# Expert stage: later scatters, and gathers just ahead of the steps that read them

## The chip, the cores and the metric

The program runs on one core of a Trainium2 chip. The metric is the device time of one execution in microseconds, less is better. TensorE multiplies matrices (in the profile PE, its weight loads PEld), VectorE (DVE) and ScalarE (ACT) move results out of the matmul banks (PSUM, eight of them, `PS`) and do the arithmetic between the matmuls, GpSimd (POOL) helps in the dense part, and SyncE (SP) issues the loads from memory. Each has its own list of instructions and they meet through semaphores only. All loads are carried by the same 16 DMA engines.

## What is computed

Two blocks in a row on 512 tokens of width 1024, all in float32. The first block has a gated recurrence, an attention and two SwiGLU layers, the second three attention branches and then a layer of experts. Only the last one is touched by the change:

```python
def expert_choice_ffn(x, w_router, w_gate_up, w_down):
    B, T, D = x.shape
    cap = EC_CAPACITY_FACTOR * T // N_EXPERTS        # 2 * 512 // 16 = 64
    logits = jnp.einsum('btd,de->bte', x, w_router, preferred_element_type=jnp.float32)
    aff = jax.nn.softmax(logits, axis=-1)
    gate, idx = lax.top_k(jnp.swapaxes(aff, 1, 2), cap)
    bidx = jnp.arange(B)[:, None, None]
    xs = x[bidx, idx]
    h = jnp.einsum('becd,edf->becf', xs, w_gate_up)
    hg, hu = jnp.split(h, 2, axis=-1)
    ye = jnp.einsum('becf,efd->becd', jax.nn.silu(hg) * hu, w_down)
    ye = ye * gate[..., None].astype(ye.dtype)
    return jnp.zeros_like(x).at[bidx, idx].add(ye)
```

Each of the 16 experts takes its 64 best tokens. Its weights are 1024 x 2048 (gate and up) and 1024 x 1024 (down), 12.6 MB for an expert, 201 MB for all. The layer's output is added to its scaled input and normalised, and that is the result.

## The kernel before

`experts_order` writes the order of the stage as a list of steps; each engine's program walks through the same list and does its part of each step, so one list sets the order on all engines. `claim` takes the PSUM bank that has been free longest, `release` says which event frees it, and a matmul that writes a claimed bank first waits for that event.

The experts run as eight pairs, i = 0 to 7, and two pairs share a group q = i // 2 of four experts. For a pair:

- `gather` (q, d): the tokens of the group's four experts, for 128 of the 1024 features, as a product of the normalised input (high part XH and low part XL, L2575 and L2576) with a one-hot matrix (the tile named PE): 16 matmuls on TensorE. VectorE scales the result into `XS[:, d]` (L2121). XS serves both pairs of the group, so for q > 0 this write waits until step `up` (2q - 1, d) has read the old one. `one_hot` (VectorE, L2114) writes the matrix of the next group.
- `up` (i, k), k = 0 to 7: 16 matmuls (L2591) with `XS[:, k]` as weights over two loads of 1 MB. Then `silu` (ScalarE) and the product (VectorE, L2127) into HG; `h_turn` transposes it (L2227) and ScalarE copies it back (L1351).
- `slot_gates` (L2605) for an even pair, the gate values of the group.
- `down` (i, k), k = 0 to 3: 16 matmuls (L2631) over two loads of 1 MB. `y_out` takes the result in a high and a low part, YOH (ScalarE) and YOL (VectorE, L2154).
- `scatter` (i, tb, h): 4 blocks of tokens by 2 halves, two matmuls each (L2660, L2661) with the transposed one-hot matrix GT, added on VectorE into X (L2148, L2150; for some L2140 is the addition of `back`). `scatter_t` makes GT: transposes of the tile PE for the group (L2227), copied by ScalarE.
- `back`, in pair 4 alone: the layer's input is transposed back and added to X.

The order around the change: pair 0 does its gathers two ahead of the `up` that reads them, two before up 0 and a pair of them behind up 1, up 3 and up 5. In pairs 1, 3 and 5 all eight gathers of the next group stand in twos behind up 1, 3, 5 and 7. The eight scatters of pair i - 1 stand between up 7 and `h_turn` of pair i. `scatter_t` stands behind down 0 of the even pairs. In pair 7 the scatters of pair 6 stand between the ups.

The weights are 196 loads that SyncE issues in their order (L1246; the last ones L1249 and L1250), 24 for a pair. There are 19 slots of 1 MB (`SL`, and the tiles C and X, which lie in other tiles' place) at first and 16 later. A load into a slot that was used waits for the `up` or `down` that read it (`ex("w", ...)`); nothing else in this list waits for other engines once the stage runs.

```python
                if j in last_in:
                    e.wait_ge(*ex("w", last_in[j] // 2))
                last_in[j] = i
```

Of the kernel before, what the change touches and what calls it, by code (L numbers as in the profile page):

```python
# [742 lines left out]
def experts_order(o, us):  # L743
# [63 lines left out]
    def gather(q, d):  # L807
        o.claim("ga", q, d)
        o.add("gather", q, d)
        o.release(("ga", q, d), "xs", q, d)  # L810

    def scatter(i, *tbs):
        for tb in tbs:
            for h in range(2):
                o.claim("sc", i, tb, h)
                o.add("scatter", i, tb, h)
                o.release(("sc", i, tb, h), "xup", "sc", i, tb, h)

    def back(c):
        if c == 0:  # L820
            o.add("ident")
        if c:
            o.claim("xb", c - 1)
            o.add("back_turn", c - 1)
            o.release(("xb", c - 1), "xup", "back", c - 1)
        if c < DC:
            o.claim("xr", c)
            o.add("back", c)
            o.release(("xr", c), "back", c)

    def carry(tb, *halves):
        for h in halves:
            o.claim("fin", tb, h)
            o.add("carry", tb, h)

    for i in range(8):
        q = i // 2
        for n in range(4):
            o.claim("h", i, n)
        if i == 0:  # L840
            o.add("one_hot", 0)
            gather(0, 0)
            gather(0, 1)
        for k in range(8):
            o.add("up", i, k)
            if i % 2 and i < 7 and k % 2:
                gather(q + 1, k - 1)
                gather(q + 1, k)
            if i == 0 and k % 2 and k < 7:
                gather(0, k + 1)  # L850
                gather(0, k + 2)
            if i == 7 and 1 <= k < 5:
                scatter(6, k - 1)
                o.add("halves", k - 1)
            elif i == 7 and k >= 5 and k < 7:
                carry(k - 5, 0, 1)
            elif i == NBACK:
                back(k)
        if i == NBACK:
            back(DC)  # L860
        for n in range(2):
            o.add("silu", i, n)
            o.release(("h", i, n), "silu", i, n)
            o.release(("h", i, 2 + n), "mul", i, n)
        if i == 0:
            o.add("alpha")
        elif i < 7:
            scatter(i - 1, *range(4))
        for half in range(2):
            o.claim("ht", i, half)  # L870
            o.add("h_turn", i, half)
            o.release(("ht", i, half), "turn", "ht", i, half)
            if i % 2 == 0 and half == 0:
                o.claim("gw", q)
                o.add("slot_gates", q)
                o.release(("gw", q), "xs", "gw", q)
        for n in range(2):
            o.claim("y", i, n)
        def y_out(n):
            o.add("y_out", i, n)  # L880
            o.release(("y", i, n), "lo", "y2", i, n)

        if i == 7:
            break
        for k in range(4):
            o.add("down", i, k)
            if i % 2 == 0 and k == 0:
                for j in range(2):
                    o.claim("gt", "e", q, j)
                    o.add("scatter_t", q, j)  # L890
                    o.release(("gt", "e", q, j), "turn", "gt", q, j)
                if q < 3:
                    o.add("one_hot", q + 1)
        y_out(0)
        y_out(1)

# [53 lines left out]
def whole_order():  # L950
    o = Order()
    rglru_order(o)
    ffn_order(o, 0, 2)
    sb_order(o)
    ffn_order(o, 1, 4)
    us = mixer2_order(o)
    o.n_dense = len(o.units)
    experts_order(o, us)
    return o
# [1867 lines left out]
```

## Time and profile before

| | us |
|---|---|
| runs of the kernel | 2118.39, 2118.40, 2119.78 |
| median | 2118.4 |
| the profiled execution, its time | 2120.52 |
| the profiled execution, its span | 2118.7 |
| TensorE busy | 2086.6 (98% of the span) |
| VectorE busy | 1023.1 (48%) |
| ScalarE busy | 750.2 (35%) |
| GpSimd busy | 146.4 (7%) |
| DMA, bytes moved | 352.09 MB |

The span runs from the first to the last instruction that the profiler saw; the time has some 1.8 us more around it. The dense part takes the first 1650 us or so, the experts run from there to 2105 us, and the last microseconds are the normalisation and the output. A busy TensorE is not one at its peak, since its matmuls are pipelined and their ends are modelled.

### The profile page before, as it was taken

The numbers are of one execution on the slowest core, as the hardware profiler recorded it, in microseconds if no ns is written. First come the engines' busy times: TensorE is split into PE (matmuls) and PEld (weight loads), VectorE is DVE, ScalarE is ACT, GpSimd is POOL, SyncE is SP. The second block draws the span as 40 slices with busy tenths as digits, with TensorE's granted clock in tenths as the row PEclk, the third lists the DMA queues.
The fourth block names the chain that finished last, engine by engine and source line by source line (L and its number), as shares of the span: only waits on it lengthen the run. The fifth ranks groups of instructions, "written<-read, shape, count | busy, mean of one in ns | idle before, by whom it ended". The sixth has DMA issues, their size and how long they took to land.

```text
span 2118.7 us, 24857 instructions
## 1 busy us (share of the span) xinstructions
PE 2086.6 (98%) x10137; PEld 1517.1 (72%) x10137; DVE 1023.1 (48%) x1515; ACT 750.2 (35%) x1076; POOL 146.4 (7%) x149
## 2 busy tenths in 40 slices
PE   9999999999999999999999999999999999999998
PEld 7878888888777778888888877777787544444433
DVE  7875433445666664434446656564464312122123
ACT  7774322323455543222334456533333100011012
POOL 0220000001000020000001010062101000000000
PEclk9999999999999999999999999999999999999999
DMA  6233223324211123233233322242236999999996
GB/s 218 75 104 110 83 83 124 100 69 121 70 60 59 61 92 105 69 123 99 82 88 119 115 60 77 60 89 72 73 110 231 401 426 412 427 427 426 426 427 275
DMA packets 88944, 352.09 MB, mean 166 GB/s; under 512 B 9472, under 2 KB 24064, under 8 KB 64512
## 3 DMA queue, kind: packets, MB, share of 16 engines
q1 hardware_dynamic: 83856, 342.48, 43.6%
q0 software_dynamic: 2192, 2.63, 1.0%
q10 hardware_dynamic: 2784, 5.41, 0.7%
q8 instruction: 81, 1.33, 0.3%
q14 instruction: 31, 0.25, 0.0%
HBM read 347.06 MB, written 2.10 MB: 165 GB/s over the span
## 4 chain that ended last, share of the span: by engine, by line
PE 86%; DVE 5%; DMA 4%; ACT 3%; issue 2%; POOL 0%; ACTq 0%; DVEq 0%; SPq 0%; POOLq 0%
PE PS L2184 20%; PE PS L2185 19%; PE PS L2186 19%; PE PS L2591 9%; PE PS L2631 4%; DMA SL<-in_wgu_dram 3%; PE PS L2227 2%; DMA SL<-in_wdn_dram 1%; DVE WL L1664 1%; PE PS L2301 1%; PE PS L2575 1%; PE PS L2325 1%; PE PS L2315 1%; PE PS L2576 1%; DVE XC L1731 1%
## 5 line engine op out<-in xcount | busy, mean ns | idle before, releaser
L2184 PE MATMUL PS<-HH,WH 128*128 128x512 f32 x1392 | 553.9, 398 | 3.0 <-DVE HL L1704 2.2
L2186 PE MATMUL PS<-HH,WL 128*128 128x512 f32 x1392 | 543.0, 390 | 0.0
L2185 PE MATMUL PS<-HL,WH 128*128 128x512 f32 x1392 | 542.6, 390 | 0.0
L1664 DVE TENSOR_TENSOR WL<-RAW,WH 128x1024 fp32r<-128x1024 f32 (+4 forms) x302 | 343.5, 1138 | 294.6 <-ACT WH L1340 293.7
L1340 ACT ACTIVATE WH<-RAW 128x1024 fp32r<-128x1024 f32 (+4 forms) x302 | 286.5, 951 | 308.5 <-PE PS L2186 278.3
L2184 PEld LDWEIGHTS PS<-HH,WH 128*128 128x128 f32 x1392 | 261.7, 188 | 69.1 <-issue 10.3
L2186 PEld LDWEIGHTS PS<-HH,WL 128*128 128x128 f32 x1392 | 261.7, 188 | 55.6
L2185 PEld LDWEIGHTS PS<-HL,WH 128*128 128x128 f32 x1392 | 262.0, 188 | 52.9 <-issue 1.0
L2591 PE MATMUL PS<-SL,XS 128*64 128x512 f32 x928 | 220.8, 595 | 6.4 <-DMA SL<-in_wgu_dram 5.8
L2591 PEld LDWEIGHTS PS<-SL,XS 128*64 128x64 f32 x928 | 70.4, 137 | 135.7 <-issue 133.7
L2186 PE MATMUL PS<-MH,WL 128*128 128x512 f32 x352 | 136.9, 389 | 0.0
L2184 PE MATMUL PS<-MH,WH 128*128 128x512 f32 x352 | 136.9, 389 | 0.0
L2185 PE MATMUL PS<-ML,WH 128*128 128x512 f32 x352 | 136.9, 389 | 0.0
L1674 DVE TENSOR_TENSOR U<-PS,RS 128x512 f32<-128x512 f32 x44 | 30.4, 691 | 106.2 <-PE PS L2186 106.2
L1449 ACT ACTIVATE MH<-U 128x512 fp32r<-128x512 f32 x44 | 27.9, 633 | 141.2 <-DVE U L1787 141.2
L1613 ACT ACTIVATE HG<-PS 128x512 f32<-128x512 f32 x8 | 4.8, 596 | 204.0 <-PE PS L2591 204.0
L2184 PEld LDWEIGHTS PS<-MH,WH 128*128 128x128 f32 x352 | 66.1, 188 | 13.8
L2186 PEld LDWEIGHTS PS<-MH,WL 128*128 128x128 f32 x352 | 66.1, 188 | 13.7
L2185 PEld LDWEIGHTS PS<-ML,WH 128*128 128x128 f32 x352 | 66.1, 188 | 13.6
L2121 DVE TENSOR_SCALAR XS<-PS,V 128x256 f32<-128x256 f32 x32 | 17.4, 544 | 116.7 <-PE PS L2576 116.7
L1776 DVE TENSOR_TENSOR X<-X,PS 128x512 f32<-128x512 f32 x56 | 38.0, 684 | 55.9 <-PE PS L2186 55.9
L1323 POOL COPY SA<-SQ 128x512 f32<-128x512 f32 x4 | 2.7, 674 | 846.9 <-ACT SQ L1372 846.9
(375 smaller groups left out, 2740.5 us busy)
## 6 DMA issues: line engine op xcount, KB each, us to landing
SL<-in_wgu_dram SPq DMA_DIRECT2D x116, 1024.0 KB, 21.8
SL<-in_wdn_dram SPq DMA_DIRECT2D x55, 1024.0 KB, 24.8
RAW<-in_w_dram SPq DMA_DIRECT2D x46, 512.0 KB, 3.4
RAW<-in_wg_dram SPq DMA_DIRECT2D x44, 512.0 KB, 3.4
RAW<-in_wu_dram SPq DMA_DIRECT2D x44, 512.0 KB, 3.4
RAW<-in_wd_dram SPq DMA_DIRECT2D x32, 384.0 KB, 3.1
RAW<-in_wqkv_dram SPq DMA_DIRECT2D x24, 512.0 KB, 3.5
RAW<-in_wd_dram SPq DMA_DIRECT2D x32, 320.0 KB, 2.9
```

What stands on the lines that cost most here:

```text
L1340: e.activation(WH[u % NSPL][:, 0:n], RAW[raw_of[u]][:, 0:n], ACT.Copy).then_inc(*whs.did("u", u))
L1449: e.activation(MH[l][:, f, :], U1[l][:, z, :], ACT.Copy).then_inc(*hi.did("m", l, half, f))
L1664: e.tensor_tensor(wl, raw, wh.bitcast(F), ALU.subtract).then_inc(*wlo.did("u", u))
L1674: e.tensor_tensor(dst, src, r, ALU.mult).then_inc(*scaled.did(*event))
L1731: e.scalar_tensor_tensor(out=XC[s][:, :], in0=XB[p][:, 1 + j:T + 1 + j], scalar=vec("cw", 8 * j + c), in1=XC[s][:, :], op0=ALU.mult, op1=A ...
L1776: e.tensor_tensor(X[:, c, :], X[:, c, :], bank(*key), ALU.add).then_inc(*xup.did(*key))
L2184: e.matmul(out, wh[:, w], xh, start=k == 0, stop=False)
L2185: e.matmul(out, wh[:, w], xl, start=False, stop=False)
L2186: m = e.matmul(out, wl[:, w], xh, start=False, stop=k == g.total - 1)
L2227: m = e.transpose(bank(*key)[:, 128 * j:128 * j + 128], src, ident)
L2591: m = e.matmul(bank("h", i, n)[64 * e2:64 * e2 + 64, :], XS[:, k, x0:x0 + 64], SL[slot(l0 + e2)][:, 512 * n:512 * n + 512], start=k == 0, ...
L2631: m = e.matmul(bank("y", i, n)[64 * e2:64 * e2 + 64, :], HT[k // 2][:, 2 * (k % 2) + f, 64 * e2:64 * e2 + 64], SL[slot(l0 + e2)][:, 1024 * ...
```

## The change

Three things move in the list of steps; no instruction is added or taken away, and the banks that are claimed shift with the order.

- Gathers: in pairs 1, 3 and 5 only gathers 0 and 1 of the next group are left, behind up 1. The other six stand in the following even pair, in twos behind its ups 1, 3 and 5, as in pair 0.
- Scatters: those of pair i - 1, for i = 1 to 6, stand behind down 0 (block 0), down 1 (block 1) and down 2 (blocks 2 and 3) of pair i, where they stood ahead of its `h_turn`.
- `scatter_t` and the next `one_hot`: for pairs 2, 4 and 6 behind down 3, where they stood behind down 0.

```diff
@@ -843,12 +843,12 @@
             gather(0, 1)
         for k in range(8):
             o.add("up", i, k)
-            if i % 2 and i < 7 and k % 2:
-                gather(q + 1, k - 1)
-                gather(q + 1, k)
-            if i == 0 and k % 2 and k < 7:
-                gather(0, k + 1)
-                gather(0, k + 2)
+            if i % 2 and i < 7 and k == 1:
+                gather(q + 1, 0)
+                gather(q + 1, 1)
+            if i % 2 == 0 and k % 2 and k < 7:
+                gather(q, k + 1)
+                gather(q, k + 2)
             if i == 7 and 1 <= k < 5:
                 scatter(6, k - 1)
                 o.add("halves", k - 1)
@@ -864,8 +864,6 @@
             o.release(("h", i, 2 + n), "mul", i, n)
         if i == 0:
             o.add("alpha")
-        elif i < 7:
-            scatter(i - 1, *range(4))
         for half in range(2):
             o.claim("ht", i, half)
             o.add("h_turn", i, half)
@@ -884,13 +882,15 @@
             break
         for k in range(4):
             o.add("down", i, k)
-            if i % 2 == 0 and k == 0:
+            if i % 2 == 0 and k == (3 if i else 0):
                 for j in range(2):
                     o.claim("gt", "e", q, j)
                     o.add("scatter_t", q, j)
                     o.release(("gt", "e", q, j), "turn", "gt", q, j)
                 if q < 3:
                     o.add("one_hot", q + 1)
+            if 0 < i < 7 and k < 3:
+                scatter(i - 1, *((0,), (1,), (2, 3))[k])
         y_out(0)
         y_out(1)
```

TensorE in pair 1, from the last scatter to the first matmul of pair 2, before. Ahead of these rows stand seven more scatters and, ahead of them, gathers 6 and 7. The counts of L2591 and L2631 are half of the matmuls, so x8 is one up or down; the two rows of L2631 are the downs 0 and 1, then 2 and 3:

```order
L2660 MATMUL PS<-YOH,GT 128x512
L2661 MATMUL PS<-YOL,GT 128x512
L2227 MATMUL PS<-C,HG 128x128 x4
L2227 MATMUL PS<-C 128x128 x4
L2631 MATMUL PS<-SL,HG 64x512 x16
L2631 MATMUL PS<-SL,C 64x512 x16
L2591 MATMUL PS<-SL,XS 64x512
```

The same place now, from the last ups of pair 1 to down 1:

```order
L2591 MATMUL PS<-SL,XS 64x512 x24
L2591 MATMUL PS<-X,XS 64x512 x8
L2227 MATMUL PS<-C,HG 128x128 x4
L2227 MATMUL PS<-C 128x128 x4
L2631 MATMUL PS<-SL,HG 64x512 x8
L2660 MATMUL PS<-YOH,GT 128x512
L2661 MATMUL PS<-YOL,GT 128x512
L2660 MATMUL PS<-YOH,GT 128x512
L2661 MATMUL PS<-YOL,GT 128x512
L2631 MATMUL PS<-SL,HG 64x512 x8
```

Nothing stands any more between the last up and the turns of HG, and the scatters have gone in between the downs.

VectorE from the end of pair 0 to the end of pair 2 (L2121 the gathers, L2127 the products, L2148 and L2150 the scatters, L2131 the gates, L2114 the one-hot matrix):

```order
-L2121 TENSOR_SCALAR XS<-PS,V 128x256 x8
+L2121 TENSOR_SCALAR XS<-PS,V 128x256 x2
 L2127 TENSOR_TENSOR HG<-HG,PS 128x512
 L2127 TENSOR_TENSOR C<-C,PS 128x512
 L2148 COPY X<-PS 128x4x128 x8
 L2154 SCALAR_TENSOR_TENSOR YOL<-PS,GA,YOH 128x512 x2
+L2121 TENSOR_SCALAR XS<-PS,V 128x256 x6
 L2127 TENSOR_TENSOR HG<-HG,PS 128x512
 L2127 TENSOR_TENSOR C<-C,PS 128x512
+L2131 COPY GA<-PS 128x2
 L2150 TENSOR_TENSOR X<-X,PS 128x4x128 x8
-L2131 COPY GA<-PS 128x2
```

Six of the eight XS writes move from pair 1 to pair 2, and the gates' copy stands ahead of the scatters. ScalarE's list and SyncE's are the same as before.

## Rows read from the trace of the kernel before

**Rows 1.** The page: span, forty slices, chain, a row of group 5.

```profile
span 2118.7 us, 24857 instructions
...
DMA  6233223324211123233233322242236999999996
GB/s 218 75 104 110 83 83 124 100 69 121 70 60 59 61 92 105 69 123 99 82 88 119 115 60 77 60 89 72 73 110 231 401 426 412 427 427 426 426 427 275
...
PE 86%; DVE 5%; DMA 4%; ACT 3%; issue 2%; POOL 0%; ACTq 0%; DVEq 0%; SPq 0%; POOLq 0%
...
L2121 DVE TENSOR_SCALAR XS<-PS,V 128x256 f32<-128x256 f32 x32 | 17.4, 544 | 116.7 <-PE PS L2576 116.7
```

**Rows 2.** Busy time by stretches; the last three columns are PEclk, DMA share, GB/s.

```profile
1750.00:1755.00 5.00, 4.79 (x26) 3.92 (x26) 5.00 (x9) 0.92 (x2) 0.00 (x0) 1.00 1.01 426
1755.00:1760.00 5.00, 5.00 (x26) 1.65 (x24) 1.47 (x3) 0.16 (x1) 0.00 (x0) 1.00 0.80 305
1760.00:1765.00 5.00, 5.00 (x26) 1.66 (x24) 0.00 (x0) 0.00 (x0) 0.00 (x0) 1.00 0.94 397
1765.00:1770.00 5.00, 5.00 (x26) 1.72 (x24) 0.55 (x1) 1.27 (x2) 0.00 (x0) 1.00 1.03 431
...
1765.00:2085.00 320.00, 311.44 (x1610) 136.87 (x1608) 67.23 (x109) 36.20 (x59) 0.00 (x0) 1.00 1.01 426
...
2005.00:2010.00 5.00, 3.79 (x19) 1.27 (x17) 0.00 (x0) 0.00 (x0) 0.00 (x0) 1.00 1.02 426
2015.00:2020.00 5.00, 3.79 (x20) 1.30 (x18) 0.00 (x0) 0.00 (x0) 0.00 (x0) 1.00 1.01 426
```

**Rows 3.** TensorE's timeline: start, duration, operation, in brackets the wait before it.

```profile
1912.91 0.63 PE L2227 MATMUL PS<-C 128*128 128x128 f32 x4 [0.96 <-ACT C L1639]
...
2003.95 3.65 PE L2591 MATMUL PS<-SL,XS 128*64 128x512 f32 x16 [0.65 <-DMA SL<-in_wgu_dram]
...
2013.79 3.65 PE L2591 MATMUL PS<-SL,XS 128*64 128x512 f32 x16 [1.32 <-DMA SL<-in_wgu_dram]
2018.65 3.65 PE L2591 MATMUL PS<-SL,XS 128*64 128x512 f32 x16 [1.21 <-DMA SL<-in_wgu_dram]
...
2082.68 0.72 PE L2227 MATMUL PS<-C 128*128 128x128 f32 x4 [0.82 <-DVE C L2127]
```

**Rows 4.** The chain that ended last, in the tail: start, duration, what.

```profile
2061.62 25.59 DMA SL<-in_wdn_dram
...
2087.34 3.65 PE PS L2631 x16
...
2092.13 5.30 PE PS L2645 x24
...
2099.02 1.89 PE PS L2645 x8
```

**Rows 5.** The same chain in pairs 0, 1 and 2.

```profile
1668.75 0.32 PE PS L2575
...
1670.84 7.02 PE PS L2591 x32
...
1713.56 6.87 PE PS L2591 x32
1720.42 0.32 PE PS L2575
...
1722.52 7.02 PE PS L2591 x32
...
1747.79 0.32 PE PS L2575
...
1753.57 0.48 PE PS L2227 x4
...
1754.73 13.95 PE PS L2631 x64
1768.68 27.47 PE PS L2591 x128
1796.15 0.43 PE PS L2660
...
1800.02 0.47 PE PS L2227 x4
1800.49 1.03 PE PS L2605 x32
...
1805.77 1.02 PE PS L2227 x8
```

**Rows 6.** Line L1246 in narrow windows: its loads, and their time to landing.

```profile
L1246 SPq DMA_DIRECT2D SL<-in_wgu_dram x2: 328/380/431, 1744.4 to 1744.8; - x2
...
DMA to landing us min/median/max: 13.0/14.0/15.0
...
L1246 SPq DMA_DIRECT2D SL<-in_wgu_dram x1: 327/327/327, 1758.4 to 1758.4; - x1
...
DMA to landing us min/median/max: 4.6/4.6/4.6
...
L1246 SPq DMA_DIRECT2D SL<-in_wgu_dram x1: 432/432/432, 1758.8 to 1758.8; - x1
...
DMA to landing us min/median/max: 6.7/6.7/6.7
...
L1246 SPq DMA_DIRECT2D SL<-in_wgu_dram x1: 327/327/327, 1761.9 to 1761.9; - x1
...
DMA to landing us min/median/max: 7.5/7.5/7.5
```

**Rows 7.** The same for later windows.

```profile
L1246 SPq DMA_DIRECT2D SL<-in_wgu_dram x8: 327/380/976, 1785.9 to 1796.6; - x8
...
DMA to landing us min/median/max: 17.8/21.1/24.3
...
L1246 SPq DMA_DIRECT2D SL<-in_wgu_dram x1: 328/328/328, 1805.8 to 1805.8; - x1
...
DMA to landing us min/median/max: 17.5/18.5/19.6
...
L1246 SPq DMA_DIRECT2D SL<-in_wgu_dram x1: 328/328/328, 1923.0 to 1923.0; - x1
...
DMA to landing us min/median/max: 18.0/18.0/18.0
```

## The prediction

> **What bounds the kernel now.** I read the page's slices first [rows 1]. TensorE is busy in nearly every slice, and the chain that ended last is 86% TensorE; that alone would say that every TensorE microsecond counts. But in the eight slices before the last, where the experts are, the DMA engines stand at 9 tenths or more and move 401 to 427 GB/s. There the chain is no longer a guide to what is scarce, so I looked at the stage in stretches of 5 us [rows 2]. From 1765 to 2085 us the mean is 426 GB/s with the DMA share at 1.01, and from 2004 us on TensorE waits for weights that have not landed: in 2005 to 2010 and in 2015 to 2020 it is busy 3.79 of 5 us, and four matmul groups in a row wait 0.65 to 1.32 us for a weight load [rows 3]. The tail hangs on that too: the chain goes through a load issued at 2061.62 that takes 25.59 us, and the step L2631 starts on it at 2087.34 [rows 4]. So the end of the program is the weight stream's end plus a tail that only starts with it. TensorE before about 2004 works off a store of landed weights; making it earlier there is worth nothing in itself. It is worth something only where its releases of slots let the stream go on.
>
> So the question is where the stream stands still for want of a free slot. After the change's first touched step (expert pair i=1, from 1713.56 on [rows 5]) there is one such place: 1755 to 1760 carries 305 GB/s and 1760 to 1765 carries 397, before and after it 426 and 431 [rows 2]. SyncE's queue says why [rows 6]: the load before the hole is issued at 1744.8 and lands 15.0 us later (1759.8), the next is issued only at 1758.4 and lands at 1763.0. It waits for the step down(1,0) to free its slot, and that step came late: up(1,7) ends at 1747.79, then stand one pair of gathers, eight scatters and the two turns, and down begins at 1754.73 [rows 5].
>
> **What the change does to the releases.** Per item, all on TensorE, durations from [rows 5]:
>
> Gathers. A pair of them is 1722.52 - 1720.42 = 2.10 us. Of the four pairs inside i=1 three move into i=2 (the same from 3 to 4 and from 5 to 6): 6.3 us leave the odd step and come back in the even one. Scatters. Eight are 3.9 us (1796.15 to 1800.02 in i=2), in i=1 they lie between the gathers and the turn at 1753.57. They move behind down 0, 1 and 2 as two, two and four, for i=1 to 6. The two scatter transposes of an even step, 1.0 us (L2227 x8 at 1805.77, [rows 5]), move behind down 3.
>
> The release that starved the stream: down(1,0) ended at 1754.73 + 3.5 = 1758.2. It loses 6.3 and 3.9 us ahead of it and ends at 1748.0. One thing is added: the scatters also covered the silu, the product and the transposes of HG. In i=7 no scatter stands there, and the second turn waits 0.82 us for VectorE's product [rows 3]; with the even steps slot_gates (1.03 us) stands between the turns and the chain shows no wait at i=0. So I add 0.8 us for each of i=1, 3 and 5: 1748.8, some 9.4 us earlier than before, and 11 us before the last issued load has landed (1759.8). From an empty queue a load takes 4.6 us from issue to landing [rows 6], so there is no hole left here.
>
> What is late next: with the same work in another order each release should be earlier or equal except for the added waits. I follow the sum: at the end of down(1,3) the scatters are done, so the lead is 6.3 - 0.8 = 5.5 us; each pair of gathers in i=2 takes 2.1 of it, so up(2,6) and up(2,7) are released 0.8 us later than before; then the eight scatters behind give 3.9 us of lead at down(2,0) and none at its end. After i=3 the lateness at the same points is 1.6, after i=5 2.4 us. The cover: the loads issued from 1785 to 1797 have 17.8 to 24.3 us until they land, the scarcest later ones are 17.5 (1806) and 18.0 us (1923) [rows 7]. Less 4.6 that is 13 us of work already queued against 2.4 us of lateness. No new hole.
>
> The new direct waits (a gather two steps ahead of the up that reads it, VectorE's XS write between them, 544 ns in [rows 1]) are already in i=0: there a pair of gathers takes 1668.75 to 1670.84, 2.09 us, the same as in i=1 where nobody reads it at once [rows 5]. I take them at zero; in i=4, where the back steps interleave with them, the nearest row is the 0.96 us wait for ScalarE [rows 3], so at most some 3 us for three pairs, hidden by the same 13 us. In i=6, where TensorE already waits for weights, it gets 6.3 us more: two ups and a pair take 7.02 + 2.10 = 9.1 us, four loads at 426 GB/s take 9.85 us (1.049 MB each), so the gathers fill part of the 1.2 us waits and delay nothing. On VectorE and ScalarE nothing is added, and SyncE's list of loads is the same.
>
> **What the hole is worth.** By bytes: (426 - 305) + (426 - 397) = 150 GB/s missing over 5 us, or 150 x 5 / 426 = 1.8 us. By landings, which is what TensorE waits for: 1759.8 to 1763.0 is 3.2 us where loads otherwise follow each other by 2.46 us, so 0.8 us. These are the two ends. The Trainium skill's page "DMA: Bandwidth & Descriptors", section "Queues, rings and completion order", says that one copy is split over up to 16 rings, each with its own engine, and so is not complete before its last part: engines that run ahead stand idle in the hole while the last ones still work. By that rule the value is 0.8 us, by the mean of the engines 1.8 us; no row here shows single engines. I take 1.0 us, nearer to the landing row, because landings release TensorE. One more row could belong to the restart: the load of 1758.8 lands at 1765.5, that of 1761.9 at 1769.4, 3.9 us apart instead of 2.46 [rows 6]. If this 1.4 us is a cost of starting again, it goes too, 2.2 to 3.2 us in all.
>
> **The sum.** Against the profiled execution (span 2118.7 us, time 2120.52, which is 1.8 us around the span and 2.1 above the median of the runs): 2120.5 - 1.0 = 2119.5. Against the median, 2118.4 - 1.0 = 2117.4 us, a change of 0.05%. A measurement of this kernel can tell about 0.2% (4.2 us) from no change, so I expect a time within that.
>
> **The rivals.**
> The hole was harmless or only moves: a small hole is paid back elsewhere, or a bank or SyncE holds the new issue. For: the byte rate before and after is already at its top. Against: nothing behind 1765 is below the mean, so what is lost there is not caught up. Time: 2118.4.
> The restart's 1.4 us belongs to it: 2118.4 - 2.7 = 2115.7. For: the long spacing stands two loads behind the hole. Against: it is one row.
> More of TensorE's lead counts, that is, TensorE and not the stream sets the end: then the change still gives nothing, since the work is the same and the added waits cost 3 x 0.8 us: 2120.8. The waits for weights in [rows 3] speak against it.
> Slower: the clock falls. TensorE gets to the store's end earlier (in i=5, since 6.3 - 2.4 = 3.9 us of work has left it by then) and waits more often in short pieces. If the granted clock drops to 1.2 GHz in the last steps, an up takes 7.0 instead of 3.5 us against loads that come every 4.9 us for two, and the lag no longer vanishes; with the tail's matmuls (3.65 + 5.30 + 1.89 + 2 us in [rows 4]) at half speed it costs some 13 us: 2131. It decides only if the low clock is there in the last ups of i=7, since a single slow one (3.5 us) is made good in three steps with 1.2 us to spare. Against: in 2005 to 2020 with TensorE at 3.79 of 5 us the granted clock is 1.00 [rows 2], and i=7 is not changed. The Trainium skill's page "TensorE: Matmul & The Clock Gate", section "HAM oscillation — how this bites in real kernels", says that matmul bursts parted by waits for DMA fall back to the half clock at each wait; that rule would make this rival the result, and no row of the weight-bound stretch shows it.
> Slower by a hole in i=4: it needs over 13 us of new waits there, for which I find no row; its price would be what exceeds them.
>
> **How the numbers follow.** Forecast (hole closed, 0.8 to 1.8 us) 60%; nothing gained 14%; restart included 15%; TensorE sets the end 5%; clock or another wait 3%; an unforeseen gain of over 4 us 3%. The runs shown spread from 2118.39 to 2119.78, 1.4 us upward. The first four lie between 2115.7 and 2120.8; the range takes the forecast's two ends, the restart's bound of 3.2 us and the spread above no change: 2115.0 to 2119.8. Within 0.2%: 94%; faster 3%; slower 3%.
>
> **What would show it.** In the changed profile the two stretches near 1755 to 1765 carry 426 GB/s; the load behind the one issued near 1744 is issued some 9 us earlier; a wait of about 0.8 us for VectorE's product appears at the second turn of i=1, 3 and 5; TensorE's first waits for weights come before 2004 and those in i=6 shrink; L2631's last wait ends near 2086.3 instead of 2087.34, and the tail from there is the same. Wrong would be a new stretch below 420 GB/s between 1765 and 2085, a granted clock under 1 there, or an end that moves by over 2 us with the same stream.

## The result and the profile after

| | before, us | changed, us |
|---|---|---|
| median of 12 runs each | 2118.79 | 2123.76 |
| lowest, highest | 2118.19, 2120.65 | 2122.41, 2126.47 |
| the profiled execution: time, span | 2120.52, 2118.7 | 2122.98, 2121.2 |

The changed kernel is 5.0 us slower: ratio 1.0022, 95% interval 1.0015 to 1.003. The prediction was 2117.4 us with a range of 2115.0 to 2119.8, so the time lies outside it and on the other side of no change.

The two profiled executions differ by only 2.5 us in span. Part of the difference lies ahead of the change: the first up of pair 1 starts at 1713.39 us in the kernel before and at 1711.83 in the changed one, 1.56 us earlier, in a stretch where both programs are the same. So I compare from there to the start of the first down of pair 7 (2083.33 before, 2086.33 now): 369.9 us before and 374.5 us now, 4.6 us more. Behind that point the changed kernel is 0.5 us shorter. Between the starts of the pairs' first ups, from TensorE's timeline:

| pair | 1 | 2 | 3 | 4 | 5 | 6 | 7, to its first down |
|---|---|---|---|---|---|---|---|
| before, us | 55.12 | 48.57 | 55.14 | 62.05 | 55.13 | 53.87 | 40.06 |
| changed, us | 50.63 | 56.40 | 50.69 | 72.20 | 50.68 | 56.40 | 37.49 |

The hole in the weight stream is gone. The same stretches as in [rows 2], the changed kernel (last three columns: granted clock, DMA share, GB/s), with two more that are read further down:

```profile
1755.00:1760.00 5.00, 5.00 (x24) 2.31 (x22) 2.31 (x4) 0.00 (x0) 0.00 (x0) 1.00 1.00 423
1760.00:1765.00 5.00, 5.00 (x26) 1.61 (x24) 1.58 (x3) 1.27 (x2) 0.00 (x0) 1.00 1.02 433
...
1765.00:2085.00 320.00, 315.75 (x1618) 135.87 (x1614) 70.29 (x113) 33.74 (x56) 0.00 (x0) 0.99 1.01 426
...
1915.00:1920.00 5.00, 2.57 (x43) 2.12 (x42) 1.96 (x4) 2.46 (x4) 0.00 (x0) 0.98 1.00 421
1920.00:1925.00 5.00, 5.00 (x20) 2.01 (x20) 0.16 (x1) 0.60 (x1) 0.00 (x0) 0.68 1.02 431
```

And the load that used to be late, which answers to [rows 6] (line L1246 in a narrow window of the changed kernel):

```profile
L1246 SPq DMA_DIRECT2D SL<-in_wgu_dram x1: 328/328/328, 1747.6 to 1747.6; - x1
...
DMA to landing us min/median/max: 13.7/13.7/13.7
```

It is issued at 1747.6, with the 1.56 us added 1749.1, where the forecast had 1748.8 and the kernel before 1758.4; it takes 13.7 us to land in place of 4.6, so there is queued work ahead of it. But TensorE no longer waits for any weights. Its waits from 1665 to 2090 us in the changed kernel (engine, line, waited for, total us, times, longest):

```profile
PE PS L2227 <- DVE C L2127: 3.3, 4, 0.8
PE PS L2227 <- DVE HG L2127: 1.5, 1, 1.5
PE PS L2227 <- ACT C L1639: 1.0, 1, 1.0
```

In the kernel before, the waits for weights alone were 6.5 us over this stage, four of them in [rows 3]; 6.0 us lie ahead of the first down of pair 7. The stream was the limit there; here it is TensorE's own list that sets the end, and every load lands before TensorE asks for it.

Where TensorE's time went is to be seen in the chain through the end of pair 1, against [rows 5] (start, duration, what; changed kernel):

```profile
1740.00 1.74 PE PS L2591 x8
...
1741.76 0.61 ACT C L1613
...
1742.39 0.70 DVE C L2127
...
1743.23 0.72 PE PS L2227 x4
1743.94 3.58 PE PS L2631 x16
1747.53 0.43 PE PS L2660
1747.96 0.24 PE PS L2661
1748.20 0.23 PE PS L2660
1748.43 0.24 PE PS L2661
1748.67 3.58 PE PS L2631 x16
...
1753.40 3.58 PE PS L2631 x16
1756.98 0.43 PE PS L2660
...
1759.05 3.58 PE PS L2631 x16
```

The first scatter matmul of each group takes 0.43 us of the chain, the next ones 0.23; each down takes 3.58, where four in a row took 13.95, or 3.49 each. From 1743.94 to the first up of pair 2 (1762.63) it is 18.69 us; before, the downs (13.95) and the scatters ahead of them (1749.91 to 1753.57, 3.66) took 17.61. That is 1.08 us more in an odd pair for work that is the same. In pair 2 it is 19.67 (1799.26 to 1818.93) against 15.06 + 3.87 = 18.93, 0.74 us more.

The second place is pair 4, in TensorE's, VectorE's and ScalarE's timeline of the changed kernel:

```profile
1915.23 0.78 ACT L1639 ACTIVATE C<-PS,LC 128x512 f32<-128x512 f32 x1 [4.24 <-PE PS L2671]
1916.15 0.63 PE L2227 MATMUL PS<-C 128*128 128x128 f32 x4 [0.96 <-ACT C L1639]
1916.82 0.69 DVE L2140 TENSOR_TENSOR X<-X,PS 128x512 f32<-128x512 f32 x1 [1.74 <-PE PS L2227]
1917.42 0.68 DVE L2127 TENSOR_TENSOR HG<-HG,PS 128x512 f32<-128x512 f32 x1
1918.25 0.72 PE L2227 MATMUL PS<-C,HG 128*128 128x128 f32 x4 [1.47 <-DVE HG L2127]
1919.95 1.13 PE L2227 MATMUL PS<-C 128*128 128x128 f32 x4
1921.02 1.12 PE L2631 MATMUL PS<-C,HG 128*64 128x512 f32 x1
1921.93 1.06 PE L2631 MATMUL PS<-C,HG 128*64 128x512 f32 x1
```

The last back step waits 0.96 us for ScalarE, as it did before. VectorE adds its result (L2140) and only then makes the product (L2127), and the turns, which nothing covers any more, wait for that, 1.47 us. Right behind these two waits the granted clock falls: 0.68 in the mean of 1920 to 1925, which holds a piece at the lower level, 1.2 GHz. The first matmuls of the down take 1.12 and 1.06 us in place of 0.59, and that down 4.67 us in place of 3.58.

**The account** (from the two traces, us of TensorE, from up(1,0) to down(7,0)). First TensorE's reserve in the kernel before, the time that it lost to the stream. Pair 6 has the same order there as pair 2 and took 53.87 us in place of 48.57; pair 7 took 40.06 us where the changed kernel, which waits for no weights, takes 37.49. That is 7.9 us: 6.0 us of waits, the rest in groups that run longer beside the waits. So without its waits the kernel before would need 362.1 us. The changed one takes 374.5, 12.4 us more: interrupted downs 3 x 1.08 + 3 x 0.74 = 5.5; the product's wait in pairs 1, 3 and 5, 3 x 0.83, less the 0.6 us that the downs waited there for HG before, 1.9; pair 4's wait 1.5; the low clock 1.5 (1.1 in the down, 0.4 in the turns); the turns, which no longer follow scatters and pay for their own first matmul, 1.4 (in pairs 1, 3 and 5 the two take 1.40 us in place of 1.11); 0.6 stays unassigned. The reserve takes up 7.9 of the 12.4, and what is left is the 4.6 between the traces (the terms are rounded); the runs have 5.0.

### The profile page after: what moved, and what is told of

It is laid out like the page before. It is cut to its first block, busy times and chain, and to the rows that moved or that the text cites. A ratio compares the mean times of both kernels' runs of the same rounds, so it can differ in the third digit from the quotient of the medians.

```text
span 2121.2 us, 24857 instructions
## 1 busy us (share of the span) xinstructions
PE 2091.8 (99%) x10137; PEld 1511.3 (71%) x10137; DVE 1025.6 (48%) x1515; ACT 750.2 (35%) x1076; POOL 146.3 (7%) x149
## 4 chain that ended last, share of the span: by engine, by line
PE 89%; DVE 5%; ACT 3%; issue 2%; DMA 1%; POOL 0%; ACTq 0%; DVEq 0%; SPq 0%; POOLq 0%
PE PS L2184 19%; PE PS L2186 19%; PE PS L2185 19%; PE PS L2591 11%; PE PS L2631 5%; PE PS L2227 2%; DVE WL L1664 1%; PE PS L2301 1%; PE PS L2660 1%; PE PS L2575 1%; PE PS L2325 1%; PE PS L2315 1%; PE PS L2576 1%; DVE XC L1731 1%; PE PS L2423 1%
## 5 line engine op out<-in xcount | busy, mean ns | idle before, releaser
L2591 PE MATMUL PS<-SL,XS 128*64 128x512 f32 x928 | 219.9, 595 | 0.0
L2591 PEld LDWEIGHTS PS<-SL,XS 128*64 128x64 f32 x928 | 68.6, 137 | 128.3 <-issue 126.4
L2184 PEld LDWEIGHTS PS<-MH,WH 128*128 128x128 f32 x352 | 66.1, 188 | 13.7
L2121 DVE TENSOR_SCALAR XS<-PS,V 128x256 f32<-128x256 f32 x32 | 17.4, 544 | 106.3 <-PE PS L2576 106.3
L1776 DVE TENSOR_TENSOR X<-X,PS 128x512 f32<-128x512 f32 x56 | 38.1, 684 | 55.9 <-PE PS L2186 55.9
L2150 DVE TENSOR_TENSOR X<-X,PS 128x512 f32<-128x512 f32 x48 | 30.4, 684 | 71.4 <-PE PS L2661 71.4
```

The source lines that it names most:

```text
L1776: e.tensor_tensor(X[:, c, :], X[:, c, :], bank(*key), ALU.add).then_inc(*xup.did(*key))
L2150: e.tensor_tensor(y, y, new, ALU.add).then_inc(*xup.did("sc", i, tb, h))
L2184: e.matmul(out, wh[:, w], xh, start=k == 0, stop=False)
L2591: m = e.matmul(bank("h", i, n)[64 * e2:64 * e2 + 64, :], XS[:, k, x0:x0 + 64], SL[slot(l0 + e2)][:, 512 * n:512 * n + 512], start=k == 0, ...
```

## Experiments

Each time is a median of 10 or 11 runs (five for the scatters alone), measured beside the kernel before on the same chip. The kernel before had a median of 2119.79, 2118.84 and 2119.18 us in the three comparisons, so a time is compared with the one of its own chip (that is what the ratio does) and not across chips. Where I give the length of "the stretch", it is the one from the first up of pair 1 to the first down of pair 7, from one trace of each kernel. From the expectations on record: pairs are numbered 0 to 7, and "the stream" is the order of weight loads.

### One half of the change at a time

The scatters alone:

```diff
-            if i % 2 and i < 7 and k == 1:
-                gather(q + 1, 0)
-                gather(q + 1, 1)
-            if i % 2 == 0 and k % 2 and k < 7:
-                gather(q, k + 1)
-                gather(q, k + 2)
+            if i % 2 and i < 7 and k % 2:
+                gather(q + 1, k - 1)
+                gather(q + 1, k)
+            if i == 0 and k % 2 and k < 7:
+                gather(0, k + 1)
+                gather(0, k + 2)
```

> Edit: from the changed kernel the gathers go back to where they were (eight in each of pairs 1, 3, 5); scatters and scatter_t stay in their new places. Theory A (the parts add up on TensorE, and the end comes late only when TensorE's sum passes the weight stream): the interrupted downs cost 1.06 us in an odd and 0.74 us in an even pair, the uncovered wait for the product 0.8 us in pairs 1, 3, 5: 7.8 us, but TensorE has 6.5 us of waits for weights in the kernel before and no gathers in pair 6, so the stream still sets the end. down(1,0) ends 3.1 us earlier, at 1755.1, so the hole of 1755 to 1765 shrinks to nearly nothing: 2116.6 to 2119 us, no slower than before. Theory B (the scatters between the downs are by themselves what costs, each microsecond on the path): 2118.8 + 5.4 + 2.4 = 2126.6, at least above 2122. Theory C (the gathers alone do the harm, by waits and the clock in pair 4): this kernel equals the one before, 2118.8.

Measured: 2126.52 us, ratio 1.0033 (1.0021 to 1.0046), worse than the whole change. Theory B's figure of 2126.6 is met, A's is missed. But B's sum is met by luck: it added 7.8 us, while TensorE got 15.9 us more (below) and its reserve took up 7.9. TensorE has no wait for weights left here either, and its stretch is 378.0 us. I had put the uncovered wait at 0.8 us a pair; it is longer when the last gathers stand right ahead of the turns. TensorE's waits from 1665 to 2090 us, and the chain at the end of pair 1:

```profile
PE PS L2227 <- DVE HG L2127: 5.4, 4, 1.5
...
1749.07 0.13 PE PS L2576
...
1749.23 0.54 DVE XS L2121
1749.77 0.60 DVE HG L2127
...
1750.51 0.73 PE PS L2227 x4
```

The product stands behind the last XS write on VectorE, and that stands behind the last gather: 5.4 us over four pairs. In pair 4 the clock stays at the lower level for longer than in the changed kernel (0.57 in 1920 to 1925, 0.75 in 1925 to 1930). Against the kernel before without its waits for weights (362.1) the stretch is 15.9 us longer; interruptions 5.5, waits 5.4 - 0.6, the clock 2.9 and the turns 1.4 explain 14.6 of them, 1.3 stays unassigned.

The gathers alone (the gather lines of the change, on the kernel before):

> Edit: the kernel before with only the gathers moved; scatters and scatter_t as before. Theory A (TensorE's sum against the stream): pair 4 costs some 3 us more (waits of 1.5 and 1.0 us and a granted clock of 0.68 in 1920 to 1925), pair 6 gets 6.3 us more, but the ups of pair 6 have room for that, and the end is set by the stream: 2116.6 to 2118.8, and the hole is closed. Theory B (scatters alone are the harm): 2116.6, the same number, with the clock at 1.00. Theory C (the gathers alone do the harm, by pair 4's waits and clock): 2122 or more, equal to the changed kernel. The profile decides between A and B by pair 4's length, 62.1 us before (1872.38 to 1934.43) and 72.1 us in the changed kernel.

Measured: 2118.07 us, ratio 0.9994 (0.9985 to 1.0003). The hole is closed, 428 GB/s in 1755 to 1760, the granted clock is 1.00 in 1915 to 1925, and waits for weights are there, 4.9 us for the ups. So the gathers do no harm to the time by themselves, not even between the back steps, and theory C falls. The scatters are where TensorE's added time comes from. A's mechanism stands for this kernel, but its expected clock drop did not come: the scatters ahead of the turns cover pair 4.

### The price of an interruption

```diff
-            if 0 < i < 7 and k < 3:
-                scatter(i - 1, *((0,), (1,), (2, 3))[k])
+            if 0 < i < 7 and k == 1:
+                scatter(i - 1, *range(4))
```

> Edit: the changed kernel with all eight scatters in one burst behind down 1 in place of two, two and four behind down 0, 1 and 2. Theory A (each place where TensorE leaves the downs for scatters and comes back costs some 0.3 us, and TensorE sets the end): two of three such places go in six pairs, 12 x 0.3 = 3.6 us: 2120.2 us, and the downs with scatters take 18.0 us in pair 1 instead of 18.7. Theory B (the interruption costs nothing, only the uncovered wait for the product counts): 2123.8, unchanged. Theory C (the gathers are the harm): 2123.8, unchanged.

Measured: 2120.33 us, ratio 1.0004 (0.9995 to 1.0013), as theory A had it. The stretch is 371.6 us, 2.9 less than in the changed kernel: five pairs are 0.72 to 0.80 us shorter each, and pair 4 is 0.85 us longer, because the clock stays low for longer there. The chain at the end of pair 1:

```profile
1743.74 7.02 PE PS L2631 x32
1750.76 0.43 PE PS L2660
1751.20 0.24 PE PS L2661
...
1754.65 7.02 PE PS L2631 x32
1761.67 3.43 PE PS L2591 x15
```

1743.74 to 1761.67 is 17.93 us against 18.69 with three interruptions: two fewer save 0.76, so 0.38 us each. It is a cost of leaving one kind of matmul for another and coming back, not of the scatters' work. The downs write 64 rows of a bank (`128*64` in the rows), the scatters 128. The Trainium skill, "TensorEngine Tiling (Array Packing)", section "Key Properties", says that a change of the tiling mode drains TensorE first. The longer first matmul agrees with it (0.43 in place of 0.23); no run here separates a drain from another cost at such a seam.

### The change at the hole alone

```diff
+            if i % 2 and i < 7 and (k % 2 if i > 1 else k == 1):
+                gather(q + 1, k - 1)
+                gather(q + 1, k)
+            if i in (0, 2) and k % 2 and k < 7:
+                gather(q, k + 1)
+                gather(q, k + 2)
...
-        elif i < 7:
+        elif 1 < i < 7:
             scatter(i - 1, *range(4))
...
+            if i == 1 and k == 1:
+                scatter(0, *range(4))
```

> Edit: the kernel before with the change at the hole alone: gathers 2 to 7 of the second group move from pair 1 to pair 2, the eight scatters of pair 0 stand in one burst behind down 1 of pair 1; all else, scatter_t too, as before. Theory A: down(1,0) ends some 9 us earlier, the hole is closed, which moved the landings by 2.2 us in the changed kernel, TensorE's sum grows by 1.5 us only and the stream sets the end: 2118.8 - 2.2 = 2116.6 us. Theory B (the end hangs on TensorE, not on the stream, and the hole has no worth): 2118.8 + 1.5 = 2120.3 us.

Measured: 2118.36 us, ratio 0.9993 (0.9984 to 1.0002). The same gathers without the scatters:

```diff
-            if i % 2 and i < 7 and k % 2:
+            if i % 2 and i < 7 and (k % 2 if i > 1 else k == 1):
                 gather(q + 1, k - 1)
                 gather(q + 1, k)
-            if i == 0 and k % 2 and k < 7:
-                gather(0, k + 1)
-                gather(0, k + 2)
+            if i in (0, 2) and k % 2 and k < 7:
+                gather(q, k + 1)
+                gather(q, k + 2)
```

> Edit: the kernel before with only gathers 2 to 7 of the second group moved from pair 1 to pair 2; scatters, scatter_t and all other pairs as before. Theory D: down(1,0) ends 6.3 us earlier, at 1752, well before the last issued load lands at 1759.8, so the hole is closed with no new wait and no interrupted downs, TensorE's sum grows by 0.2 us: 2118.8 - 1.8 to 2.2 = 2116.6 to 2117.0 us, as good as the kernel with both moves at pair 1. Rival (the hole has no worth at the end): 2118.8.

Measured: 2118.84 us, ratio 0.9998 (0.9989 to 1.0007), the same median as the kernel before. Both have whole streams at 1755 to 1765 (426 and 434 GB/s in the first five microseconds), both wait for weights later (4.2 and 4.8 us for the ups), and neither can be told from the kernel before. By the medians the hole was worth between nothing and 1.7 us at the end: these are the differences in the five kernels that close it and still wait for weights (the gathers alone, the two here, and two further down). The forecast's 1.0 is within that and not confirmed by it. The traces narrow it a little. The stretch is 369.1 to 369.2 us in four of these five kernels and 369.8 in the one with both moves at pair 1, against 369.9 in the kernel before and 370.1 in the one further down that keeps the hole. That is 0.7 to 1.0 us for the hole, with one case of 0.2 or 0.3, near the 0.8 that the forecast had from the landings; each is a single trace. The medians can't show it, since that first up starts anywhere from 1711.2 to 1714.4 us in the traces of the twelve kernels, though nothing ahead of it was changed.

### Is TensorE the bound?

Both kernels without the low part of the scatters of pairs 0 to 6:

```diff
-                    e.matmul(out, hot, YOH[:, cols], start=i < 7, stop=False, skip_group_check=True)
-                    e.matmul(out, hot, YOL[:, cols], start=False, stop=True, skip_group_check=True).then_inc(
-                        *ex.did("sc", i, tb, h))
+                    low = i == 7
+                    m = e.matmul(out, hot, YOH[:, cols], start=i < 7, stop=not low, skip_group_check=True)
+                    if low:
+                        m = e.matmul(out, hot, YOL[:, cols], start=False, stop=True, skip_group_check=True)
+                    m.then_inc(*ex.did("sc", i, tb, h))
```

> Edit: the changed kernel without the low parts in the scatters of pairs 0 to 6 (the L2661 matmul of 56 scatters is left out, so the sums lack the low part); order, loads, and the work of the other engines stay. It takes 56 x 0.23 = 12.9 us from TensorE. Theory D (in the changed kernel TensorE's own sum sets the end: it waits for no weights there, while the last loads land 0.9 to 1.0 us earlier than before, counted from the first expert load): TensorE falls below the stream and the stream sets the end, with the hole closed: 2118.8 - 2.2 = 2116.6 us, and waits for weights come back. Rival (the stream, or something behind it, sets the changed kernel's end): 2123.8, unchanged.

> Edit: the kernel before without the same 56 matmuls (the sums lack the low part of the scatters of pairs 0 to 6). Theory D: the stream sets this kernel's end, so 12.9 us less on TensorE are worth only what they do to the hole: down(1,0) ends 1.8 us earlier, which closes about half of it: 2117 to 2118.8 us. Rival (TensorE sets the end in both): 2106 us.

Measured: the changed kernel falls from 2123.76 to 2117.82 us (ratio 0.9993, 0.9984 to 1.0002), the kernel before stays at 2118.49 (0.9998, 0.9989 to 1.0007), with a hole that is only a little smaller (303 and 421 GB/s in its two stretches), not half as the expectation had it. The same 12.9 us of matmuls are worth some 6 us in the one and nothing that can be measured in the other. TensorE's waits for weights from 1665 to 2090 us, first of the changed kernel cut short, then of the kernel before cut short:

```profile
PE PS L2591 <- DMA SL<-in_wgu_dram: 4.8, 7, 1.4
```

```profile
PE PS L2591 <- DMA SL<-in_wgu_dram: 11.9, 13, 1.4
```

The work that was taken away turned into waits. This settles the main question: the stream bounded the kernel before, TensorE bounds the changed one.

### Pair 4

```diff
         if i == 0:
             o.add("alpha")
+        elif i == 4:
+            scatter(i - 1, *range(4))
...
-            if 0 < i < 7 and k < 3:
+            if 0 < i < 7 and i != 4 and k < 3:
```

> Edit: the changed kernel, with the eight scatters of pair 3 put back ahead of the turns of pair 4; the other pairs as changed. Theory E (the clock falls in pair 4 because nothing stands any more between the last back step and the turns: waits of 0.96 us for ScalarE and 1.47 us for VectorE's product, which stands behind the addition of back, follow each other): both the 1.47 us wait and the drop of the granted clock go, pair 4 is shorter by 1.9 us for these and 0.85 us for the uninterrupted downs, and as TensorE sets the end the kernel is at 2123.8 - 2.8 = 2121.0 us. Rival (the gathers between the back steps cause the drop): the clock falls at 1915 to 1925 as before, and only 0.85 us are won: 2122.9.

Measured: 2118.52 us, ratio 0.9996 (0.9987 to 1.0005): one pair of six put back takes the whole loss away. The wait and the clock drop are gone (this kernel's lines stand two further down):

```profile
PE PS L2229 <- DVE C L2129: 3.3, 4, 0.8
PE PS L2229 <- ACT C L1641: 1.0, 1, 1.0
...
1915.00:1920.00 5.00, 4.08 (x20) 3.48 (x21) 3.41 (x6) 1.86 (x3) 0.00 (x0) 1.00 1.01 426
1920.00:1925.00 5.00, 5.00 (x55) 2.98 (x56) 3.32 (x7) 1.19 (x2) 0.00 (x0) 1.00 1.02 429
```

Theory E holds: the gathers between the back steps are still there and the clock stays at its upper level. The gain is larger than the 2.8 us that I expected. By the traces 4.3 us go (374.5 to 370.2 for the stretch): 1.5 for the wait, 1.5 for the clock, 1.0 for the downs and scatters, 0.3 for the turns; I had read the wait and the clock as 1.9 together. The medians moved by 5.2 us, from comparisons on different chips. Part of the 0.9 between the two can be the clock, whose cost is not the same in each execution: the turns, the gates and the first downs of pair 4 lose 1.5 us by it in the trace of the changed kernel and 2.9 to 3.2 us in those of the four other kernels where it falls. That it makes up the difference is not shown. There is no wait for weights left here, so TensorE still sets the end, some 1 us above the 369.1 to 369.2 that the whole stream takes.

### The place of the last gathers, and both repairs

```diff
-            if i % 2 and i < 7 and k == 1:
-                gather(q + 1, 0)
-                gather(q + 1, 1)
-            if i % 2 == 0 and k % 2 and k < 7:
+            if i % 2 and i < 7 and (k % 2 if i == 5 else k == 1):
+                gather(q + 1, k - 1)
+                gather(q + 1, k)
+            if i % 2 == 0 and i != 6 and k % 2 and k < 7:
                 gather(q, k + 1)
                 gather(q, k + 2)
```

> Edit: the changed kernel with the last group's gathers back in pair 5 (all eight behind ups 1, 3, 5 and 7) in place of pair 6; the other groups' gathers, the scatters and scatter_t as changed. Theory D (TensorE's sum sets the end and has no wait for weights left from pair 1 on): moving 6.3 us of the same work from one pair to the one before changes nothing by itself. Only the product's wait behind the last pair of gathers in pair 5 gets longer, from 0.8 to 1.5 us: 2123.8 to 2125 us. Rival (the harm of the moved gathers is that they load pair 6, where there used to be waits of 5.8 us for weights): 2118 to 2120 us.

Measured: 2124.55 us, ratio 1.0025 (1.0016 to 1.0035). The gathers in pair 6 are not the harm. Moved back to pair 5 they make the product's wait there longer, 2.8 us in two places where the changed kernel has 1.5 in one; pairs 5 and 6 together are 0.4 us longer. The stretch is 376.5 us, 2.0 more than in the changed kernel, and the other 1.7 us are pair 4's, whose steps are the same: the clock was low for longer in this execution (0.50 in 1920 to 1925).

```diff
+        elif i == 4:
+            scatter(i - 1, *range(4))
...
-            if 0 < i < 7 and k < 3:
-                scatter(i - 1, *((0,), (1,), (2, 3))[k])
+            if 0 < i < 7 and i != 4 and k == 1:
+                scatter(i - 1, *range(4))
```

> Edit: the changed kernel with both repairs: scatters in one burst behind down 1 in pairs 1, 2, 3, 5 and 6, and ahead of the turns in pair 4. Theory D: TensorE's stretch from the first up of pair 1 to the first down of pair 7 was 374.5 us in the changed kernel, 3.8 us (one burst) and 4.3 us (pair 4 covered) go, 366.4 us, which is below the 369 us of the stream: waits for weights come back and the time is the stream's, 2117 to 2118.8 us, no better than with either the gathers alone or pair 4 covered alone. Rival (each microsecond of TensorE still counts): 2123.8 - 8.1 = 2115.7 us.

Measured: 2118.5 us, ratio 0.9995 (0.9986 to 1.0004). The two repairs do not add up: waits for weights are back (1.8 us for the ups) and the stretch is 369.2 us, the stream's. Of all versions none is faster than the kernel before beyond its interval.

## Why the prediction was wrong

- **What bounds the kernel before.** Right: the stream. 12.9 us less on TensorE are worth nothing measurable there.
- **"TensorE before about 2004 works off a store of landed weights; making it earlier there is worth nothing in itself."** Right for earlier, and the prediction stopped there. Later is not free: it is covered only as far as TensorE's reserve goes (see the cover, below).
- **The hole and its cause.** Right: it closed, and the late load is issued within 0.3 us of the forecast place. Its worth at the end could not be told from none by the medians, which leave 0 to 1.7 us open; the traces speak for the forecast's lower bound of 0.8. The term "from an empty queue" was read loosely: the load of 1758.4 was issued 1.4 us before the last one landed, so its 4.6 us are not all its own.
- **The restart's 1.4 us.** The 3.9 us between two landings is no mark of the hole. The trace of the kernel before has another such step, 3.9 us up to 1952.3, and that of the gathers alone, without a hole, has steps of 4.1 and 3.9 us, where 2.44 is the median.
- **"With the same work in another order each release should be earlier or equal except for the added waits."** This step failed. The order itself costs: 0.38 us for a place where the downs are left and taken up again, by the one burst in pair 1, and 5.5 us over the three such places of six pairs (0.36 a place in an odd pair, 0.25 in an even one, where a first scatter at 0.43 us stood before too). The turns, which no longer follow scatters, add 1.4 us. The rows that bounded it stood in [rows 5]: the first L2660 there takes 0.43 us, the next piece begins only then, and the first L2575 takes 0.32. I read these as the price of a matmul and not of a seam, and took zero.
- **The added wait of 0.8 us in pairs 1, 3 and 5.** Right in size (0.83), from the row of pair 7.
- **Pair 4.** This step failed. I looked there for a cost of the gathers between the back steps and found 0.96 us. The cost is where the scatters left: the product stands on VectorE behind the addition of back, so the turns wait 1.47 us, and the granted clock falls behind the two waits, another 1.5 us in the changed kernel's trace. The prediction had the clock as a rival, but placed it in the last ups of pair 7 and priced it at 13 us.
- **The cover.** This is what turned wrong terms into a wrong sign. I set 2.4 us of lateness against 13 us of queued loads. That cover protects the stream from running dry; it says nothing on whether TensorE keeps up with it. TensorE's own reserve is what it loses to the stream, 7.9 us ahead of pair 7's first down. Against that the change put 12.4. The rival "TensorE sets the end" had this mechanism, with 2.4 us as its price and 5% as its chance.
- **"In i=6 the gathers fill part of the waits and delay nothing."** Only for a TensorE that is on time. It reached pair 6 at 1992.60 on the chain (before 1989.57, and 1.56 us of offset on top): 4.6 us later, not 3.9 us earlier as I had worked out, and all of its room there was used up.

## What to carry to other kernels

When two engines run nearly level, write down each one's reserve over the whole stage, and sum the change against the smaller one: cover for the transfers (loads in the queue) and cover for TensorE (the time that it loses to its waits for loads) are different accounts, and a move can close a hole in one and overdraw the other. Work that is moved out from between a producer and its consumer leaves the wait that it covered, so look at every instance, above all the one where the product has something else ahead of it in its engine's queue. Small matmul groups of another shape put between long runs have a price at each seam, which shows in the first matmul of the group.

## What the runs showed of the hardware that was not expected

Leaving the downs for scatters and coming back costs 0.38 us of TensorE each time in pair 1, with nothing to wait for (17.93 us with one such place against 18.69 with three).

The granted clock of TensorE fell to its lower level in pair 4 in all five kernels with no scatters ahead of that pair's turns: 0.68 in 1920 to 1925 in the changed kernel, 0.57 with the scatters alone moved, 0.50 with the last gathers back in pair 5, 0.64 in 1915 to 1920 with one burst, 0.50 there with the low parts left out. It stayed at 1.00 there in all seven that kept them. Ahead of each fall stood two waits of 0.96 and 1.47 us with small matmuls between them; in [rows 3] four waits of up to 1.32 us with full ups between them had no fall behind them. What the fall costs differs, 1.5 us in one trace and 2.9 to 3.2 us in four. The Trainium skill, "TensorE: Matmul & The Clock Gate", section "HAM oscillation — how this bites in real kernels", tells of such falls in a kernel whose bursts of matmuls are shorter than the waits for loads between them. The turns here are like that, 0.63 us between the two waits, though these are waits for ScalarE and VectorE; the ups of 3.65 us in [rows 3] are not, so the prediction was wrong to read the section as a forecast for them.
